# A two-layer forward pass: the merged attention and recurrence stage with its work dealt out differently over four places

## The reference, cut to what matters

```python
# 8 heads of 64: stick-breaking attention
z = q @ k.T * 64 ** -0.5
log_beta, log_keep = log_sigmoid(z), where(valid, log_sigmoid(-z), 0)
log_tail = cumsum(log_keep, reverse=True) - log_keep
o = where(valid, exp(log_beta + log_tail), 0) @ v      # then an RMS norm per head
# 4 heads of 128: gated recurrence, in chunks of 128 rows
scores = einsum('td,sd,tsd->ts', q, k, decay)          # decay = exp of a difference of running sums
o = scores @ v + (q * exp(bc)) @ state                 # then an RMS norm per head and a gate
```

## The kernel before, in words

| | place 0 | place 1 | place 2 | place 3 |
|---|---|---|---|---|
| TensorE | Z(i) | R(i-1) blocks 0, 1 | SO(i-2) | R(i-1) blocks 2, 3, 4 |
| VectorE | scores(i) | subtract 0, 1; head sums | logits(i) | subtract 2, 3, 4 |
| ScalarE | weights(i-2), Abs, Exp | Log | copy of SO(i-2) | |
| GpSimd | | | head norm(i-3), blocks' sums(i) | square(i-2) |

## Time and profile before

### The profile page before, as it was taken

One profiled execution on the slowest core, in us unless ns is written; L12 is line 12 of the kernel. 1 busy time (PEld: TensorE's weight loads), 2 busy tenths in 40 slices (PEclk: granted clock), 3 DMA queues, 4 the chain that ended last, 5 costly groups with the idle time before them and its releaser, 6 DMA issues.

```text
span 1876.1 us, 18635 instructions
## 1 busy us (share of the span) xinstructions
PE 1575.6 (84%) x7428; PEld 1031.5 (55%) x7428; DVE 745.4 (40%) x1201; ACT 333.6 (18%) x558; POOL 266.1 (14%) x311
## 2 busy tenths in 40 slices
PE   5996999897899697788699978998788887887882
PEld 4685888785788442333588866767633332332330
DVE  6899645526355511111732338875320000000003
ACT  3310100115200210000311155751110000000001
POOL 0102003300000130110200014762020000000001
PEclk9998999999999798899799988988899998999986
DMA  4232122220135799999322200004789999999993
GB/s 168 76 110 70 64 94 90 90 71 20 46 138 213 283 370 413 427 428 397 148 90 83 96 1 1 1 1 173 313 313 430 429 429 430 429 430 429 431 408 152
DMA packets 54818, 412.02 MB, mean 220 GB/s; under 512 B 13888, under 2 KB 15168, under 8 KB 25936
## 3 DMA queue, kind: packets, MB, share of 16 engines
q1 hardware_dynamic: 45008, 394.05, 52.3%
q0 software_dynamic: 9728, 16.81, 2.4%
HBM read 402.40 MB, written 25.20 MB: 228 GB/s over the span
## 4 chain that ended last, share of the span: by engine, by line
PE 53%; DMA 26%; DVE 10%; ACT 4%; POOL 3%; issue 2%; SPq 2%; POOLq 0%; DVEq 0%; ACTq 0%
PE bank L1428 33%; PE bank L647 8%; DMA arena<-in_expert_gate 5%; DMA arena<-in_expert_in 5%; DMA arena<-in_expert_up 5%; DMA arena<-in_expert_down 5%; PE bank L657 3%; DMA ring<-in_expert_up 2%; DMA arena<-in_expert_out 1%; DVE arena L2149 1%; PE bank L1543 1%; DVE top L2148 1%; DVE ring_low L2044 1%; PE bank L1420 1%; ACT misc L1800 1%
## 5 line engine op out<-in xcount | busy, mean ns | idle before, releaser
L647 PE MATMUL bank<-arena 128*64 128x512 f32 x960 | 286.1, 656 | 76.8 <-DMA arena<-in_expert_up 22.4
L647 PEld LDWEIGHTS bank<-arena 128*64 128x64 f32 x960 | 96.2, 151 | 249.1 <-issue 246.5
L647 PE MATMUL bank<-ring,arena 128*64 128x512 f32 x576 | 182.4, 624 | 25.1 <-DMA ring<-in_expert_up 9.5
L895 DVE TENSOR_TENSOR arena<-misc,bank 128x256 f32<-128x256 f32 (+1 forms) x32 | 17.7, 554 | 443.4 <-PE bank L647 305.4
L2043 DVE CAST ring_high<-ring 128x2048 fp32r<-128x2048 f32 x60 | 75.9, 1265 | 262.1 <-DMA ring<-in_stream_a 158.5
L2044 DVE TENSOR_TENSOR ring_low<-ring,ring_high 128x2048 fp32r<-128x2048 f32 x60 | 140.8, 2347 | 2.1
L657 PE MATMUL bank<-arena 128*64 128x512 f32 x448 | 116.1, 603 | 20.7 <-issue 11.8
L1428 PE MATMUL bank<-ring_low,xn_high 128*128 128x512 f32 x288 | 113.3, 393 | 0.0
L1428 PE MATMUL bank<-ring_high,xn_low 128*128 128x512 f32 x288 | 112.6, 391 | 0.0
L1428 PE MATMUL bank<-ring_high,xn_high 128*128 128x512 f32 x288 | 112.6, 391 | 0.0
L647 PEld LDWEIGHTS bank<-ring,arena 128*64 128x64 f32 x576 | 60.4, 144 | 90.0 <-issue 90.0
(11 more groups left out here) (373 smaller groups left out, 2845.6 us busy)
## 6 DMA issues: line engine op xcount, KB each, us to landing
ring<-in_stream_a SPq DMA_DIRECT2D x42, 1024.0 KB, 5.0
arena<-in_expert_gate SPq DMA_DIRECT2D x20, 2048.0 KB, 28.4
arena<-in_expert_up SPq DMA_DIRECT2D x20, 2048.0 KB, 28.1
arena<-in_expert_in SPq DMA_DIRECT2D x19, 2048.0 KB, 26.9
arena<-in_expert_down SPq DMA_DIRECT2D x18, 2048.0 KB, 28.9
ring<-in_expert_up SPq DMA_DIRECT2D x12, 2048.0 KB, 32.0
ring<-in_expert_down SPq DMA_DIRECT2D x12, 2048.0 KB, 29.7
ring<-in_expert_gate SPq DMA_DIRECT2D x12, 2048.0 KB, 31.0
```

The source lines that it names most:

```text
L647: last = nc.tensor.matmul(h[side * SLOTS:(side + 1) * SLOTS, :], tokens[:, k, side * SLOTS:(side + 1) * SLOTS], w[:, k * 512:(k + 1) * 512 ...
```

## The change

The two sides of `stick_out` and of the sums change places, and the sums are made from the last block on. After the change the pieces stand like this:

| | place 0 | place 1 | place 2 | place 3 |
|---|---|---|---|---|
| TensorE | Z(i) | SO(i-2) | R(i-1) blocks 4, 3, 2 | R(i-1) blocks 1, 0 |
| VectorE | scores(i) | head sums | subtract 4, 3, 2 | subtract 1, 0; logits(i) |
| ScalarE | weights(i-2), Abs, Exp | Log, copy of SO(i-2) | | |
| GpSimd | blocks' sums(i-1) | | square(i-2), head norm(i-3) | |

The blocks' sums of head 0 are made in turn 1, place 1. The products of the recurrence's heads 2 and 3 move from steps 13 and 17 to 10 and 18. At the end (turn 8), output 6 comes ahead of the last sums R(7), and weights 7 move from place 1 to place 3.

```diff
-PRODUCTS_AFTER = (6, 13, 17)
+PRODUCTS_AFTER = (6, 10, 18)
 def sums_blocks(i, place):
-    if not 1 <= i < SBH + 1:
-        return ()
-    return {1: range(NT2), 3: ()}.get(place, ()) if i == SBH else {1: (0, 1), 3: (2, 3, 4)}.get(place, ())
+    return {2: (4, 3, 2), 3: (1, 0)}.get(place, ()) if 1 <= i < SBH + 1 else ()
...
# second_block_units, TensorE and ScalarE: SO(i - 2) and its copy
-            if place == 2 and i >= 2:
+            if place == 1 and i >= 2:
...
# SyncE, before a load of output weights
-                    sp.wait_ge(psum_filled2, U2.filled(("R", SBH - 1, NT2 - 1)))
+                    sp.wait_ge(psum_filled2, U2.filled(("R", SBH - 1, 0)))
...
# ScalarE
             def stick_weights(g):
-                wait_read2(act, ("R", g, NT2 - 1))
+                wait_read2(act, ("R", g, 0))
-                    if (i, place) == (SBH, 1):
+                    if (i, place) == (SBH, 3):
                         stick_weights(SBH - 1)
...
# VectorE
-                    if place == 2 and 1 <= i < SBH or (i, place) == (1, 0):
+                    if place == 3 and 1 <= i < SBH or (i, place) == (1, 0):
                         stick_logits(i if place else 0)
                     if (i, place) == (SBH, 3):
+                        head_sums(SBH - 2)
                         out_sums(HGH - 1)
-                    if place == 1 and i >= 3:
+                    if place == 1 and 3 <= i < SBH + 1:
                         head_sums(i - 3)
...
# GpSimd
+                    if place == 0 and 2 <= i < SBH + 1 or (i, place) == (1, 1):
+                        sums_of_blocks(i - 1)
+                    if place == 2 and 2 <= i < SBH + 1:
+                        head_square(i - 2)
                     if (i, place) == (SBH, 2):
                         out_square(HGH - 1)
-                    if place == 3 and 2 <= i < SBH + 1:
-                        head_square(i - 2)
+                    if place == 2 and 3 <= i < SBH + 1:
+                        head_norm(i - 3)
                     if (i, place) == (SBH, 3):
+                        head_norm(SBH - 2)
                         out_norm(HGH - 1)
-                    if place == 2 and i >= 3:
-                        head_norm(i - 3)
-                    if place == 2 and 1 <= i < SBH or (i, place) == (1, 0):
-                        sums_of_blocks(i if place else 0)
```

More of the change, by code:

```diff
@@ L269, in norm_orders @@
                     sums.append(("state", h - 1))
+            if place == 2 and 2 <= i < SBH + 1:
+                squares.append(("stick", i - 2))
             if (i, place) == (SBH, 2):
                 squares.append(("state", HGH - 1))
-            if place == 3 and 2 <= i < SBH + 1:
-                squares.append(("stick", i - 2))
             if (i, place) == (SBH, 3):
-                sums.append(("state", HGH - 1))
-            if place == 1 and 3 <= i < SBH + 2:
+                sums += [("stick", SBH - 2), ("state", HGH - 1)]
+            if place == 1 and 3 <= i < SBH + 1:
                 sums.append(("stick", i - 3))
```

## The result

The changed kernel takes 1881.08 us (median of 9 runs, 1878.92 to 1884.47) against 1870.97 us before in the same comparison: the ratio is 1.0044 with a 95% interval of 1.0023 to 1.0065, so it is 8 us slower by the ratio (the medians differ by 10). A second comparison with 12 runs gave 1.0045 (1.0024 to 1.0066). The forecast was 1875.5 us in a range from 1865 to 1881.5: the direction of the sum was right, its size about 5 us too small, and the measured median lies only 0.4 us inside the upper end of the range.

A forecast was written before the change was run, and what follows sets the result against it. TensorE was taken as the bound, VectorE close behind, in a stage whose length moves the program's end. Clean terms -1.5 - 1.1 + 0.3 = -2.3 us plus 5.4 for half clock gave +3.1, so 1875.5 us, range 1865 to 1881.5.

The forecast's parts named there:

- The ring: VectorE and ScalarE work in sequence between two scores: 18.2 us, some 16 before, against TensorE's turn of 18.24.
- a sign of being wrong: TensorE busy for more than 95% of the middle turns would mean the VectorE and ScalarE sequence is short.
- Contention: Rival, chance 0.15: GpSimd lengthens VectorE's products in places 3 and 0, 1.6 us a turn, 9.6 over six turns.
- TensorE freed of its stalls: Rival, chance 0.20: TensorE stays the bound and loses idle times and one half-clock stretch; -9 us, 1863.5.
- The stall that the change was seen to remove: Turn 6: 2.46 us of idle TensorE, then 10.2 us at half clock in which 5.1 us of work went missing.
- The clock: Half-clock stretches after three TensorE idle times, each charged with a half, plus turn 1's; together 5.4 us.
- The end: From scores 7 to the first transposes: 24.9 + 8.1 = 33.0 us against 32.70 before, clock charged apart.
- Turn 1 to 2: Scores 1 to scores 2: first blocks' sums start 2 us later, mostly covered; 24.5 us against 26.0.
- Turns 2 to 7: Scores 2 to scores 7: 103.4 us against 104.5 before, a change of -1.1 at full clock.
- its own case: The forecast with its clock losses, chance 0.45: 0 to +6 us, 1872.5 to 1878.5.
- The turn 6 price: GpSimd's out_norm, 3.8 us, stands ahead of the blocks' sums in turn 6; TensorE waits some 2.3 us.
- Products at 10 and 18: Moving the recurrence's products costs nothing: at step 10 their wait runs as long as that for the next level exponential.

The follow-up runs named there:

- the filled kernel: Changed kernel with the last block's two matmuls of R(2) made twice and those of step 27 three times; ratio 0.9999 to the kernel before.
- the second filling of the kernel before: Kernel before with block 2 of R(5) made three times, beside head 1's diagonal products made three times; ratio 1.0004 for both.
- the run with both edits together: Changed kernel with place 3's level exponential ahead of the Log and out_norm behind the blocks' sums; ratio 1.0017 to the kernel before.

## Why the prediction was right, and where its size was not

*The ring* is right as a mechanism and a little too long as a sum. At full clock its turns were forecast as 19.3, 20.7 and 22.4 us and measured as 18.4, 19.9 and 22.3. The order is seen in the profile, and taking the level exponential out of it (logits at place 2) makes these turns 17.9, 19.2 and 20.4. But the forecast named as a sign of being wrong that TensorE is busy for more than 95% of the middle turns, and in turn 2 to 3 it is, for 18.25 of 18.40 us, as in turn 4 to 5 of the filled kernel (18.09 of 18.60). There the ring and TensorE are equally long; in turns 3 to 4 and 5 to 6 (90 and 93%) TensorE is held, mostly by VectorE's products. Part of the excess is in how the sum was made: VectorE operations overlap in the profile (products of 0.42 start 0.34 apart), which a sum of durations counts twice.

Scores 2 to 7 can be taken apart: 95.0 us with the logits at place 2, 5.0 more with the ring and TensorE kept busy (100.0 with the fillings), 4.8 more with the idle times left in (104.8). The filled kernel carries 1.7 us of extra work there, so the split is good to about 2 us.

*Contention*, the rival of 15 in 100, did not come in the ring, whose products take 0.42. It came where the sums stood at place 2. *TensorE freed of its stalls* did not come. The stall that the change was seen to remove did go, with its stretch, and a like one came in turn 3 (2.18 us, where 2.6 were forecast).

*The clock* has the right mechanism, shown in both kernels by the fillings, and a charge that was too low. I charged half a stretch for each of three idle times. Two of the three places had a stretch in both profiles, turn 3 (2.18) and the end (2.53); turn 6 with 1.73 had none. The first cost 4.7 us, not 1.6, for the ring hid nothing of it.

*The end* is the term that was mis-sized most: 24.9 + 8.1 = 33.0 plus 2.0 for the clock, against 37.9. The step that failed is again the clock. R(7) was to start 18.7 us after scores 7; with TensorE kept at full clock it started after 19.3, in the changed kernel after 22.8. So SO(6) and HO(3) at half clock cost 3.5 us, where 2.0 were charged, and the late sums 0.6. From the last subtraction to the transposes it took 8.8 us (8.1 forecast), with SO(7) at 3.81 instead of 3.2.

*What was luck.* The forecast of +3.1 us looks met by the first profile, where the stage is 3.2 us longer, but the parts are not. Turn 1 to 2, with its clock, was to give -0.65 and gave -2.4. Turns 2 to 7 were to give -1.1 plus 2.6 for the clock, +1.5; they gave -4.5 with the fillings and 4.8 more without, +0.3. The end was to give +2.3 and gave +5.2. Errors of both signs cancel. And the runs, at +8, lie above the range that the forecast gave to its own case (0 to +6), where only the rival of contention had been priced, and that did not come.

*The turn 6 price* of `out_norm` ahead of the sums was there (1.73 for 2.3), but it is no loss by itself: with it gone, TensorE waited ahead of step 22 for ScalarE. *Turn 1 to 2* gained 2.4 where 1.5 was forecast. *Products at 10 and 18* cost nothing, as forecast.

One name in the text ahead was wrong: the rows from 1204.5 to 1223, headed as turn 6, are of turn 5 (scores 5 end at 1207.1). The sum was made by the times and is not touched; but the second filling of the kernel before followed the name, stood in R(5) and missed.

*Open.* The profiles put 3.2 and 6.1 us of the loss into the stage, the runs show 8.3. The other versions show the same: in all twelve comparisons the runs' difference from the kernel before is above the stage's difference in the profiles, by 0.6 to 8.0 us. The kernel before took 1878 us in both of its profiled executions, where its medians are 1871 to 1876, and the granted clock, which is on record for every run, was 0.927 and 0.928 in these two against a median of 0.930 (all but one from 0.922 to 0.938, the longer runs tending to the lower clock). One stretch of 10.2 us at half clock is worth 0.0027 of the clock and 5.1 us (an estimate: half of 10.2 over the span of 1876.1). So it fits that many executions of the kernel before have one stretch less than its two profiles show; where it would be missing, no run can tell.

## What to carry to other kernels

When a wait is taken out of one engine's order, write down the whole ring through all engines that the new order closes, with the operations that used to run beside each other; a move that puts two of them in a row costs although no engine is busy for longer. Short idle times of TensorE are charged twice where half clock follows them, so 2 us in such a place can be worth up to 7 (an estimate: 2.18 us and half of a stretch of 10.2; filling the one in turn 3 gave back 4.7); filling an idle time with repeated matmuls is a cheap test of it. Durations of neighbouring rows overlap, so such a ring is better summed from start to start. And when one queue's order is changed, ask for each operation in front of the critical one what it waits for itself.

## What the runs showed of the hardware that was not expected

Idle times of 2.0 to 2.6 us between busy stretches of TensorE went with half clock, which began at them or within 3 us, in most places and in several programs: 2.18 us with 17.1 and 20.5 us of it, 2.46 and 2.53 with 10.2, 2.06 with 3.4. Those of 2.16, 2.26, 2.38 and 2.39 us did not, nor did one of 2.51. Of the idle times from 1.5 to 1.8 us one was followed by half clock (1.62 us in the run with both edits together, 6.8 us of it), the others not. So the length of an idle time alone does not tell here whether half clock follows.

A kernel with 3.6 us more of matmuls in two such places was faster by 8 us. A GpSimd operation of 1.04 us took 2.80 beside a VectorE operation with two inputs of 1792 columns.
